# Context columns normed and projected ahead of the latents at three stage entries, with buffers moved to make room

## The chip, the cores and the metric

The kernel runs on one core of one Trainium2 chip. The metric is the device time of one execution in microseconds (us); lower is better. A core has five engines with a queue each: TensorE (PE, matmuls), VectorE (DVE), ScalarE (ACT), GpSimd (POOL) and SyncE (SP, here the stream of weights). Engines meet through semaphores; each works through its own queue in order.

## The reference, cut to what matters

Two models run one after the other. The first block is two layers of five attention branches and ends in a norm; its output `x` (512 tokens, 1024 features) is the "latent" input of the second. The second block also has a "context" of 256 tokens, and every one of its stages begins with the same modulated norm of both:

```python
def _modulate(x, shift, scale):
    return _rms(x) * (1 + scale) + shift

for layer in range(DEPTH):
    h_lat = _modulate(xl, mod_l[0], mod_l[1])
    h_ctx = _modulate(xc, mod_c[0], mod_c[1])
    if layer % 2 == 0:
        y_lat, y_ctx = _conformer_mlstm_mixer(h_lat, h_ctx, ...)   # h @ ab_w_in
    else:
        y_lat, y_ctx = _mla_mixer(h_lat, h_ctx, ...)               # h @ mla_w_in
    xl = xl + mod_l[2] * y_lat
    xl = xl + mod_l[5] * _conv_ffn(_modulate(xl, mod_l[3], mod_l[4]), ffn_w_in[layer], ...)
    if not last:
        xc = xc + mod_c[2] * y_ctx
        xc = xc + mod_c[5] * _conv_ffn(_modulate(xc, mod_c[3], mod_c[4]), ...)
```

The context is known from the start; it changes after the first mixer and after the first FFN, and its projections need its own norm only. So at the entry of the conformer mixer ("AB"), of the first FFN and of the MLA mixer, the context columns do not depend on the last latents.

## The kernel before

Activations lie feature-major: 8 tiles (`k`, KT = 8) of 128 features, each with 768 columns: 256 of context (`BOTH[0]`), then 512 of latents (`BOTH[1]`, `LATENT`). Products in split precision are three matmuls for each pair of tiles (`mm`, L308 to L310): high by high, low by high, high by low. A weight chunk comes by DMA (L416), is cast by ACT to its high half (`Weights.round`, L385) and gets its low half from POOL (`low_parts`, L403, event `weights_low`). PE waits for that event before it uses the chunk. There are NSPLIT = 3 split buffers, so chunk t is cast once chunk t-3 has been used. `round(key, ahead)` casts everything up to `ahead` chunks (AHEAD = 2) beyond the key's, and it stands in ACT's queue where the code calls it: a chunk is never cast before ACT has come to that call.

A stage entry goes like this. DVE adds the residual of the last feature tile (L2058, L2371, L3814), ACT squares it (L492), DVE adds squares (`add_vector`, L500), PE sums over partitions with a matrix of ones in plain fp32 (`sums_tensor`, L307), ACT takes Ln and Exp (L528, L532), DVE does a Newton step (L541 to L550). Then per tile `k`, context first and latents second: DVE scales (`scaled_vector`, L559), ACT makes the high half (`apply_scalar`, L600), DVE the low half (`low_vector`, L571). `apply_scalar` calls `round` for the four chunks ("parts") of the first group after k = 1, 3, 5 and 7. PE follows with `project_group` (or the same loop in `latents_tensor`): three outputs side by side, tile by tile, both column ranges, in four parts of two tiles. At AB the three are gates, g0 and a0, and the next projection is q0; at the FFN they are gate 0, value 0 and gate 1, and the next is value 1; at MLA they are two tiles of the key-value latent and the rope keys (`mla_kr`), and the next is the first query tile (`mla_cq` 0).

What ACT does next in its queue matters too. In `conformer_scalar` it is the sigmoid of g0, an Exp and a Ln of the gates, and then `round` of q0. In `ffn_in_scalar` the first `round` is that of value 1, and it stands at the end of f = 1:

```python
    for f in range(FT):
        ...
        if f > 1:
            g.weights.round(k)
        ... # copy of gate f, wait for the taps of DVE, gelu
        if f > 0:
            g.weights.round(("ffn_value", l, f))
```

In `latents_scalar` it is that of `mla_cq` 0, behind the copies of the first latent and of the rope keys.

PE's accumulators are 8 banks; `claim` waits until the former owner is drained. The final norm of the first block and the latent norm of AB follow each other: the final norm's scaled tiles are squared one by one and summed in 8 fp32 products. The context norm of AB is summed during the last out projection of the first block (`merge_out`), at d = 5. The out products of the FFN (`ffn_out_tensor`) run over the context columns first, then over the latents.

Of the kernel before, what the change touches and what calls it, by code (L numbers as in the profile page):

```python
# [451 lines left out]
class Norm:  # L452
    def __init__(self, key, x, nk, lo, hi, gain, out, sq, dim, shift=None, func=ACT.Identity, rounded=None,
                 added=False, paired=False):
# [67 lines left out]
def root_scalar(g, n):  # L522

    act, S = g.act, g.event
    r = n.sq[:, 1, 0:n.n]
    for m in g.after(act, S("summed").at(n.key)):
        act.wait_ge(*m)
    act.activation(r, g.bank(("sum", n.key), n.nb)[:, 0:n.n], ACT.Ln, bias=g.eps, scale=1.0 / n.dim).then_inc(  # L528
        *S("logarithm").up(act, n.key))
    for m in g.after(act):  # L530
        act.wait_ge(*m)
    act.activation(r, r, ACT.Exp, scale=-0.5).then_inc(*S("root_guessed").up(act, n.key))  # L532


def root_vector(g, n):

    dve, S = g.dve, g.event
    t, r, total = n.sq[:, 0, 0:n.n], n.sq[:, 1, 0:n.n], g.bank(("sum", n.key), n.nb)[:, 0:n.n]
# [14 lines left out]
def scaled_vector(g, n, k):  # L553
# [5 lines left out]
    dve.scalar_tensor_tensor(o, n.x[:, k, n.lo:n.hi], n.gain(k), n.sq[:, 1, 0:n.n], ALU.mult,  # L559
# [27 lines left out]

def apply_scalar(g, *norms, rounds=(), ahead=AHEAD):

    act, S = g.act, g.event  # L590
    for k in range(norms[0].nk):
        for n in norms:
            for m in g.after(act, S("normed").at((n.key, k))):
                act.wait_ge(*m)
            if isinstance(n.out, Split):
                o, high = n.rounded[k % 2][:, 0:n.n], n.out[:, k, n.lo:n.hi].high
                if n.shift is None:
                    act.copy(high, o).then_inc(*S("normed_high").up(act, (n.key, k)))
                else:
                    act.activation(high, o, n.func, bias=n.shift(k)).then_inc(*S("normed_high").up(act, (n.key, k)))  # L600
            else:
                o = n.out[:, k, n.lo:n.hi]
                act.activation(o, o, n.func, bias=n.shift(k)).then_inc(*S("shifted").up(act, (n.key, k)))
        if k % 2 and k // 2 < len(rounds):
            g.weights.round(rounds[k // 2], ahead)

# [1430 lines left out]
def merge_out_scalar(g, l):  # L2037
    act, S, n, last = g.act, g.event, next_norm(g, l), l == DEPTH - 1
    act.preload_act_table_set("natural_log_exp_and_others")
    for d in range(KT):  # L2040
# [6 lines left out]
        if last and d == 5:  # L2047
            root_scalar(g, context_norm(g))
    square_scalar(g, n, KT - 1, [S("drained").at(("merge_out", l, KT - 1))])


def merge_out_vector(g, l):
    dve, S, n = g.dve, g.event, next_norm(g, l)
    for d in range(KT):
# [7 lines left out]
        if l == DEPTH - 1 and d == 5:  # L2062
            root_vector(g, context_norm(g))

# [45 lines left out]
def first_tensor(g):  # L2110
# [26 lines left out]
    sums_tensor(g, final_norm(g), Turn(0, 8))  # L2137
    g.reach(pe, "first_block")


def first_scalar(g):
# [50 lines left out]
    root_scalar(g, n)  # L2192
    for k in range(KT):
# [89 lines left out]
def project_group(g, key, keys, turn, cols, name, lead, x, spans, each, per=2):  # L2283

    pe, n = g.pe, len(keys)
    width = len(cols) // n
    turn.i += turn.i % 2
    for k in keys:
        g.claim(k, turn.next(2), 2)
    for part in range(KT // per):  # L2290
        w, c = g.weights.piece((key, part), name, lead, rows_of(per, part * per * P), cols, split=True)
        for k in range(per):
            kk = part * per + k
            for i, out in enumerate(keys):
                for lo, hi in spans:
                    for m in g.after(pe, each(lo, kk)):
                        pe.wait_ge(*m)
                    done = mm(g, g.wide(out, lo, hi), w[:, k, i * width:(i + 1) * width], x[:, kk, lo:hi], kk == 0,
                              kk == KT - 1)
                if kk == KT - 1:  # L2300
                    done.then_inc(*g.event("projected").up(pe, out))
        if part < KT // per - 1:
            done.then_inc(*g.event("projected").up(pe, (key, part)))
            g.weights.used(c, "projected", (key, part))
        else:
            g.weights.used(c, "projected", keys[-1])
# [10 lines left out]
def modulations(g, l, name, room, shift, scale, with_ctx=True, latent_first=False, added=False):  # L2317
    t, out = g.t, []
    sides = ((1, t.xc, 0, CTX, room.sq_ctx, room.rounded_ctx), (0, t.x, CTX, SEQ, room.sq_lat, room.rounded))
    for side, x, at, n, sq, rounded in sides[0 if with_ctx else 1:]:  # L2320
        out.append(Norm((name, l, side), x, KT, 0, n, lambda k, side=side: mod(g, l, scale, k, side),
                        room.h2[:, :, at:at + n], sq, D_MODEL, rounded=rounded, added=added,
                        shift=lambda k, side=side: mod(g, l, shift, k, side)))
# [37 lines left out]

def residual_vector(g, key, l, which, d, with_ctx=True):
# [21 lines left out]

def conformer_tensor(g, l, norms, turn):
# [8 lines left out]
    project_group(g, "ab_first", [key("gates"), key("g", 0), key("a", 0)], turn,  # L2394
                  np.concatenate([GATES4, ab_cols("g", 0), ab_cols("a", 0)]), "ab_w_in_2", (0,), t.ab.h2, BOTH, each)
# [684 lines left out]

def ab_out_tensor(g, l, turn):
    S = g.event
    for d in range(2, KT):
        project_wide(g, ("ab_out", d), turn, np.arange(d * P, (d + 1) * P), "ab_w_out_2", (0,), g.t.mixed_split, BOTH,
                     lambda lo, k: S("mixed_low").at(k))


def ab_out_scalar(g, l):
# [3 lines left out]
    for d in range(KT):  # L3092
# [3 lines left out]
    residual_squares_scalar(g, norms, KT - 1, [S("drained").at(("ab_out", KT - 1))])  # L3096


def ab_out_vector(g, l):
    dve, S = g.dve, g.event  # L3100
    for d in range(KT):
        residual_vector(g, ("ab_out", d), l, 2, d)
        residual_adds_vector(g, ffn_norms(g, l), d)

# [26 lines left out]
def latents_tensor(g, l, norms, turn):  # L3131
# [7 lines left out]
    turn.i += turn.i % 2  # L3139
    for key, _ in LATENTS:  # L3140
        g.claim(key, turn.next(2), 2)
    for part in range(KT // 2):
        w, c = g.weights.piece(("mla_first", part), "mla_w_in_2", (0,), rows_of(2, part * 2 * P), LATENT_COLS, split=True)
        for k in range(2):
            kk = part * 2 + k
            for key, at in LATENTS:
                for lo, hi in BOTH:
                    for m in g.after(pe, each(lo, kk)):
                        pe.wait_ge(*m)
                    done = mm(g, g.wide(key, lo, hi), w[:, k, at:at + P], t.mla.h2[:, kk, lo:hi], kk == 0, kk == KT - 1)  # L3150
                if kk == KT - 1:
                    done.then_inc(*S("projected").up(pe, key))
# [1186 lines left out]
```

## Time and profile before

| | us |
|---|---|
| median of 3 runs | 3566.45 (3566.43 to 3570.71) |
| the profiled execution | 3567.14 |
| its span in the trace | 3565.8 |
| PE busy | 3361.5 (94%) |
| DVE busy | 1729.6 (49%) |
| ACT busy | 1281.4 (36%) |
| POOL busy | 1021.5 (29%) |

The time of an execution lies 1.3 us above its span. PE's share of busy time is an average over stages; the stage entries are where it is idle. Durations of matmuls in the rows are latencies: they overlap, and the pace is the distance from start to start.

### The profile page before, as it was taken

What the parts mean: (1) busy time and instruction counts of PE and PEld (TensorE: products, weight loads), DVE (VectorE), ACT (ScalarE), POOL (GpSimd) and SP (SyncE); (2) the same over time, 40 slices, a digit from 0 to 9 for tenths busy, and PEclk for the clock granted to TensorE, in tenths of its full rate; (3) what the DMA queues carried; (4) which work ended last, traced back from release to release, by engine and by line L of the source; (5) the groups of instructions that cost most, each with busy time, mean ns of one, the idle gap of its engine ahead of it and who ended that gap; (6) DMA issues with size and microseconds to landing.
All of it is one profiled execution on the core that took longest, in us unless ns stands there. A gap on an engine that the chain in (4) does not pass through costs nothing.

```text
span 3565.8 us, 44523 instructions
## 1 busy us (share of the span) xinstructions
PE 3361.5 (94%) x17208; PEld 2635.6 (74%) x17208; DVE 1729.6 (49%) x3130; ACT 1281.4 (36%) x2198; POOL 1021.5 (29%) x443
## 2 busy tenths in 40 slices
PE   8999999999999999999899889999998988889999
PEld 6677777776867777677687577888987656667877
DVE  5347335434137633534588755222455655543234
ACT  4333323323333332332433443222333445543332
POOL 3123121133302222113235732223453100034443
PEclk9999999999999999999999999999999999999999
DMA  5532121122552122113222001211332110022232
GB/s 180 195 114 83 39 84 60 58 98 104 178 214 73 52 74 76 54 52 133 70 72 77 1 24 54 71 60 62 109 121 74 43 43 1 1 66 95 95 100 77
DMA packets 88340, 288.48 MB, mean 81 GB/s; under 512 B 10048, under 2 KB 20672, under 8 KB 87360
## 3 DMA queue, kind: packets, MB, share of 16 engines
q1 hardware_dynamic: 86832, 274.77, 22.4%
q10 hardware_dynamic: 1296, 10.87, 0.8%
q8 instruction: 136, 2.23, 0.3%
q14 instruction: 76, 0.62, 0.1%
HBM read 281.40 MB, written 4.19 MB: 80 GB/s over the span
## 4 chain that ended last, share of the span: by engine, by line
PE 55%; DVE 6%; ACT 2%; issue 2%; POOL 0%; DVEq 0%; ACTq 0%; POOLq 0%
PE psum L308 14%; PE psum L309 14%; PE psum L310 14%; PE psum L307 11%; PE psum L3448 1%; DVE mla_cols L3537 1%; PE psum L3436 1%; PE psum L1144 1%; DVE h_low L571 1%; DVE padded L2564 0%; DVE ml_weights L2957 0%; PE psum L3414 0%; DVE rounded L559 0%; ACT mla_probs L3493 0%; ACT k_feat L3484 0%
## 5 line engine op out<-in xcount | busy, mean ns | idle before, releaser
L403 POOL TENSOR_TENSOR weights_low<-weights_loaded,weights_high 128x1024 fp32r<-128x1024 f32 (+2 forms) x380 | 910.4, 2396 | 2478.3 <-ACT weights_high L385 2449.1
L308 PE MATMUL psum<-h_high,weights_high 128*128 128x512 f32 (+1 forms) x2400 | 919.9, 383 | 40.7 <-DVE h_low L571 26.5
L309 PE MATMUL psum<-h_low,weights_high 128*128 128x512 f32 (+1 forms) x2400 | 888.5, 370 | 0.0
L310 PE MATMUL psum<-h_high,weights_low 128*128 128x512 f32 (+1 forms) x2400 | 887.7, 370 | 0.0
L308 PEld LDWEIGHTS psum<-h_high,weights_high 128*128 128x128 f32 x2400 | 458.1, 191 | 140.3 <-issue 55.8
L385 ACT CAST weights_high<-weights_loaded 128x1024 fp32r<-128x1024 f32 (+2 forms) x380 | 392.6, 1033 | 462.2 <-PE psum L310 387.5
L309 PEld LDWEIGHTS psum<-h_low,weights_high 128*128 128x128 f32 x2400 | 458.4, 191 | 84.6 <-issue 11.9
L310 PEld LDWEIGHTS psum<-h_high,weights_low 128*128 128x128 f32 x2400 | 457.3, 191 | 78.2
L3804 DVE TENSOR_TENSOR act_low<-ffn_act,act_high 128x512 fp32r<-128x512 f32 (+1 forms) x66 | 142.2, 2154 | 138.5 <-ACT act_high L3774 138.4
L308 PE MATMUL psum<-act_high,weights_high 128*128 128x512 f32 (+1 forms) x528 | 187.8, 356 | 8.4 <-DVE act_low L3804 6.2
L310 PE MATMUL psum<-act_high,weights_low 128*128 128x512 f32 (+1 forms) x528 | 187.5, 355 | 0.0
L309 PE MATMUL psum<-act_low,weights_high 128*128 128x512 f32 (+1 forms) x528 | 187.4, 355 | 0.0
L884 ACT ACTIVATE sig<-psum 128x512 f32<-128x512 f32 x80 | 47.8, 597 | 365.5 <-PE psum L310 341.5
L3686 DVE TENSOR_SCALAR psum<-ffn_row,second 128x770 f32<-128x770 f32 (+1 forms) x44 | 41.7, 949 | 280.5 <-ACT ffn_row L3658 280.4
L307 PE MATMUL psum<-gate,weights_loaded 128*128 128x512 f32 x320 | 155.2, 608 | 3.5 <-ACT gate L656 2.5
L308 PE MATMUL psum<-weights_high,h_high 128*128 128x512 f32 (+3 forms) x432 | 143.7, 333 | 11.2 <-DVE h_low L569 6.1
L309 PE MATMUL psum<-weights_low,h_high 128*128 128x512 f32 (+3 forms) x432 | 141.7, 328 | 0.0
L310 PE MATMUL psum<-weights_high,h_low 128*128 128x512 f32 (+3 forms) x432 | 141.5, 328 | 0.0
L1214 ACT ACTIVATE x<-x,softmax_cols 128x256 f32<-128x256 f32 (+4 forms) x192 | 98.5, 513 | 82.7 <-DVE softmax_cols L1248 77.9
L308 PEld LDWEIGHTS psum<-act_high,weights_high 128*128 128x128 f32 x528 | 100.6, 191 | 23.4 <-issue 5.8
L905 DVE SCALAR_TENSOR_TENSOR sig<-sig,psum 128x512 f32<-128x512 f32 x64 | 44.0, 688 | 149.7 <-PE psum L307 137.3
L2527 DVE SCALAR_TENSOR_TENSOR psum<-padded,second,psum 128x256 f32<-128x256 f32 (+1 forms) x180 | 112.1, 623 | 6.4
(447 smaller groups left out, 5201.2 us busy)
## 6 DMA issues: line engine op xcount, KB each, us to landing
weights_loaded<-stream_dram SPq DMA_DIRECT2D x472, 512.0 KB, 3.3
weights_loaded<-stream_dram SPq DMA_DIRECT2D x80, 128.0 KB, 3.2
weights_loaded<-stream_dram SPq DMA_DIRECT2D x24, 384.0 KB, 3.0
weights_loaded<-stream_dram SPq DMA_DIRECT2D x8, 272.0 KB, 5.5
x<-x_dram SPq DMA_DIRECT2D x4, 512.0 KB, 6.5
arena_mem<-mem_dram ACTq DMA_DIRECT2D x2, 1024.0 KB, 6.7
x<-x_dram ACTq DMA_DIRECT2D x1, 2048.0 KB, 7.7
x_kept_dram<-x ACTq DMA_DIRECT2D x1, 2048.0 KB, 8.7
```

The source lines that it names most:

```text
L307: return pe.matmul(out, a, b, start=start, stop=stop)
L308: pe.matmul(out, a.high, b.high, start=start, stop=False)
L309: pe.matmul(out, a.high, b.low, start=False, stop=False)
L310: return pe.matmul(out, a.low, b.high, start=False, stop=stop)
L385: act.copy(self.high[t % NSPLIT][:, 0:size], self.raw[c % NRAW][:, 0:size]).then_inc(*g.event("weights_high").up(act, c))
L403: pool.tensor_tensor(self.low[s][:, 0:size], raw[:, 0:size], self.high[s][:, 0:size], ALU.subtract).then_inc(*g.event("weights_low").up(po ...
L884: act.activation(g.t.sig[g.sigs.place[key]][:, :], g.bank(key), ACT.Tanh, scale=0.5).then_inc(*S("drained").up(act, key))
L905: dve.scalar_tensor_tensor(dst, s[:, :], 1.0, g.bank(key), ALU.add, ALU.mult).then_inc(*S("drained").up(dve, key))
L1214: act.activation(p[:, h, 0:u.keys], p[:, h, 0:u.keys], ACT.Exp, bias=c[:, 4 + h:5 + h], scale=SCALE, accum_out=None if u.keep is not None ...
L2527: dve.scalar_tensor_tensor(acc, t.up[:, c, at + j:at + j + size], cw[:, j:j + 1], acc, ALU.mult, ALU.add).then_inc(*S("convolved").up(dve, ...
L3686: dve.tensor_scalar(x, r[:, base:base + n], cw[:, 0:1], g.small.ffn_b[l][f], ALU.mult, ALU.add).then_inc(*S("tapped").up(dve))
L3804: dve.tensor_tensor(t.ffn[l].part[i % NPART].low[:, 0:n], t.ffn[l].act[:, f, lo - lo0:lo - lo0 + n], t.ffn[l].part[i % NPART].high[:, 0:n] ...
```

## The change: what it does

At the entries of AB, FFN 0 and MLA the context's norm, its scaling and the first CTX_AHEAD = 3 of 4 parts of the first projection group are moved ahead of the latents' norm. `project_group` becomes a class `Group` with `context(part)`, `latent(part)` and `both(part)`. At AB, DVE scales 6 context tiles in `merge_out` at d = 6, and PE runs `context(0)` before the final norm's sum, `context(1)` and `context(2)` before the latents' sum. At the FFN, the last two out projections of AB are split by side: context columns of both, half of the latents of one, the context's sum, and the rest. At MLA, all 8 context tiles are normed while the FFN's out products of the latents run; bank 7 is held back there for f = 0 and 1 so that the context's sum can use it. In the three places ACT calls `round` after k = 1 and k = 3 of the latents, and once or twice earlier; the calls after k = 5 and 7 are gone. The root of the MLA's context gets a buffer of its own, the fences of PE at `ab_done` and `ffn_done` become marks, and buffers are moved. The second FFN keeps its form.

```diff
+def applied_scalar(g, n, k):       # the body of apply_scalar for one norm and tile
...
+def applied_vector(g, steps):
+    for i, (n, k) in enumerate(steps):
+        scaled_vector(g, n, k)
+        if i:
+            low_vector(g, *steps[i - 1])
+    low_vector(g, *steps[-1])
+CTX_AHEAD = 3
+def early(n):
+    return [(n, k) for k in range(2 * CTX_AHEAD)]
+def late(ctx, lat):
+    return [(lat, k) for k in range(2 * CTX_AHEAD)] + [(n, k) for k in range(2 * CTX_AHEAD, KT) for n in (ctx, lat)]
@@ merge_out_scalar
         if last and d == 5:
             root_scalar(g, context_norm(g))
+        if last and d > 5:
+            for k in range(3 * d - 18, 3 * d - 15):
+                applied_scalar(g, context_norm(g), k)
@@ merge_out_vector
         if l == DEPTH - 1 and d == 5:
             root_vector(g, context_norm(g))
+        if l == DEPTH - 1 and d == 6:
+            applied_vector(g, early(context_norm(g)))
@@ first_tensor
-    sums_tensor(g, final_norm(g), Turn(0, 8))
+    turn = Turn(0, 6)
+    turn.i = 2
+    g.ab_group, sums = ab_group(g, turn), Turn(6, 2)
+    g.ab_group.context(0)
+    sums_tensor(g, final_norm(g), sums)
     g.reach(pe, "first_block")
+    for part in range(1, CTX_AHEAD):
+        g.ab_group.context(part)
+    sums_tensor(g, latent_norm(g), sums)
@@ first_scalar
     root_scalar(g, n)
+    g.weights.round(("ab_first", 0))
@@ class Group
+    def context(self, part):
+        g, pe = self.g, self.g.pe
+        w, _ = self.weights(part)
+        for out, at in zip(self.keys, self.ats):
+            self.claim(out)
+            for k in range(2):
+                kk = 2 * part + k
+                for m in g.after(pe, self.each(0, kk)):
+                    pe.wait_ge(*m)
+                mm(g, g.wide(out, 0, CTX), w[:, k, at:at + P], self.x[:, kk, 0:CTX], kk == 0, kk == KT - 1)
+    def rest(self):
+        for part in range(CTX_AHEAD):
+            self.latent(part)
+        for part in range(CTX_AHEAD, KT // 2):
+            self.both(part)
@@ ab_out_tensor: d = 6 and 7
+def ab_out_apart_tensor(g, turn):
+    ctx, lat = ffn_norms(g, 0)
+    opened, sums = [], Turn(0, 2)
+    for i in range(2):
+        opened.append(ab_out_open(g, AB_APART + i, turn))
+        ab_out_side(g, AB_APART + i, opened[i], BOTH[0], range(KT))
+    ab_out_side(g, AB_APART, opened[0], BOTH[1], range(KT // 2))
+    sums_tensor(g, ctx, sums)
+    ab_out_side(g, AB_APART, opened[0], BOTH[1], range(KT // 2, KT))
+    ab_out_side(g, AB_APART + 1, opened[1], BOTH[1], range(KT))
+    g.reach(g.pe, "ab_done")
...
+    g.ffn_group.context(0)
+    sums_tensor(g, lat, sums)
+    g.reach(g.pe, ("modulated_ffn", 0))
+    for part in range(1, CTX_AHEAD):
+        g.ffn_group.context(part)
+def ab_out_apart_scalar(g):
...
+    root_scalar(g, ctx)
+    square_scalar(g, lat, KT - 2, [S("drained").at(("ab_out", KT - 2))])
+    g.weights.round(first[0], 1)
+    for n, k in early(ctx)[:AB_EARLY]:
+        applied_scalar(g, n, k)
+    square_scalar(g, lat, KT - 1, [S("drained").at(("ab_out", KT - 1))])
+    g.weights.round(first[0])
+    for n, k in early(ctx)[AB_EARLY:]:
+        applied_scalar(g, n, k)
+AB_EARLY = 3
+def ab_out_apart_vector(g):
...
+    applied_vector(g, early(ctx)[:AB_EARLY])
+    residual_side_vector(g, ("ab_out", KT - 1), ("ab_out", KT - 1), 0, 2, KT - 1, 0)
+    applied_vector(g, early(ctx)[AB_EARLY:])
@@ latents_tensor
+    group.context(0)
+    sums_tensor(g, norms[1], Turn(6, 2))
+    g.reach(pe, "modulated_mla")
+    for part in range(1, CTX_AHEAD):
+        group.context(part)
+    group.rest()
     queries(0)
@@ ffn_out_tensor
+            late = with_ctx and side == 0
+            for d in range(KT - 1 if late and f < 2 else KT):
...
+            if late and f == 0:
+                sums_tensor(g, mla_modulations(g)[0], Turn(KT - 1, 1))
@@ ffn_out_scalar
+        if with_ctx and s == FT:
+            root_scalar(g, norms[1])
+        if with_ctx and 0 <= s - FT - MLA_CTX < KT:
+            applied_scalar(g, norms[1], s - FT - MLA_CTX)
     if with_ctx:
-        squares(0)
+        squares(0, [("mla_first", 1), ("mla_first", 2)])
@@ second_scalar
     root_scalar(g, latent_norm(g))
-    apply_scalar(g, context_norm(g), latent_norm(g), rounds=group_parts("ab_first"))
+    for n, k in late(context_norm(g), latent_norm(g)):
+        applied_scalar(g, n, k)
+        if n.key[2] == 0 and k in (1, 3):
+            g.weights.round(("ab_first", k // 2))
     fence_scalar(g, "modulated_ab")
     g.weights.note("conformer")
     conformer_scalar(g, 0)
...
-    modulate_scalar(g, mla_modulations(g), group_parts("mla_first"))
+    ctx, lat = mla_modulations(g)
+    root_scalar(g, lat)
+    for k in range(KT):
+        applied_scalar(g, lat, k)
+        if k in (1, 3):
+            g.weights.round(("mla_first", k // 2))
@@ ffn_scalar
-    modulate_scalar(g, ffn_norms(g, l), group_parts(("ffn_first", l)))
+    first = group_parts(("ffn_first", l))
+    if with_ctx:
+        ctx, lat = ffn_norms(g, l)
+        root_scalar(g, lat)
+        for n, k in late(ctx, lat):
+            applied_scalar(g, n, k)
+            if n is lat and k in (1, 3):
+                g.weights.round(first[k // 2])
+    else:
+        modulate_scalar(g, ffn_norms(g, l), first)
```

## Rows read from the trace of the kernel before

**Rows 1.** Timeline, PE, AB entry: start, us, engine, operation, count [idle before <- releaser].

```profile
1747.02 1.96 PE L307 MATMUL psum<-merged,common 128*128 128x512 f32 x4 [1.67 <-DVE merged L500]
1754.39 9.13 PE L307 MATMUL psum<-squares,common 128*128 128x512 f32 x16 [5.41 <-ACT squares L492]
1769.27 0.55 PE L308 MATMUL psum<-h_high,weights_high 128*128 128x256 f32 x1 [5.76 <-DVE h_low L571]
...
1797.71 0.28 PE L308 MATMUL psum<-h_high,weights_high 128*128 128x256 f32 x1
```

**Rows 2.** Timeline, PE, FFN 0 entry.

```profile
2164.26 3.23 PE L307 MATMUL psum<-squares,common 128*128 128x512 f32 x4
2173.22 0.55 PE L308 MATMUL psum<-h_high,weights_high 128*128 128x256 f32 x1 [5.73 <-DVE h_low L571]
...
2201.39 0.28 PE L308 MATMUL psum<-h_high,weights_high 128*128 128x256 f32 x1
```

**Rows 3.** Timeline, PE, MLA entry.

```profile
2737.25 1.23 PE L307 MATMUL psum<-squares_ctx,common 128*128 128x256 f32 x4 [2.60 <-DVE squares L500]
2738.27 3.49 PE L307 MATMUL psum<-squares,common 128*128 128x512 f32 x4
2747.50 0.55 PE L308 MATMUL psum<-h_high,weights_high 128*128 128x256 f32 x1 [5.73 <-DVE h_low L571]
...
2777.13 0.40 PE L308 MATMUL psum<-h_high,weights_high 128*128 128x512 f32 x1
```

**Rows 4.** Windows of 1 us: stretch, PE, PEld, DVE, ACT, POOL, granted clock, DMA, GB/s.

```profile
1775.00:1776.00 1.00, 1.00 (x6) 0.86 (x5) 0.93 (x3) 0.50 (x1) 0.00 (x0) 0.73 0.31 33
2178.00:2179.00 1.00, 1.00 (x7) 0.91 (x6) 1.00 (x1) 0.00 (x0) 0.81 (x1) 0.85 0.00 0
2751.00:2752.00 1.00, 1.00 (x5) 0.76 (x4) 0.96 (x2) 0.96 (x2) 0.74 (x1) 0.63 0.00 0
```

**Rows 5.** Timeline, PE in the AB group, full clock.

```profile
1775.67 0.28 PE L308 MATMUL psum<-h_high,weights_high 128*128 128x256 f32 x1
...
1776.03 0.40 PE L308 MATMUL psum<-h_high,weights_high 128*128 128x512 f32 x1
...
1776.71 0.28 PE L308 MATMUL psum<-h_high,weights_high 128*128 128x256 f32 x1
```

**Rows 6.** Timeline, DVE, before and in the AB entry.

```profile
1736.49 1.50 DVE L544 TENSOR_TENSOR ml_q<-ml_q 128x256 f32<-128x256 f32 x1
...
1745.46 0.69 DVE L2058 SCALAR_TENSOR_TENSOR x<-psum,x 128x512 f32<-128x512 f32 x1 [4.02 <-PE psum L310]
...
1767.33 0.48 DVE L559 SCALAR_TENSOR_TENSOR rounded_ctx<-context,mods,ml_q 128x256 f32<-128x256 f32 x1
```

**Rows 7.** Timeline, POOL: low halves of a 768- and a 1024-column chunk.

```profile
1735.55 2.15 POOL L403 TENSOR_TENSOR weights_low<-weights_loaded,weights_high 128x768 fp32r<-128x768 f32 x1 [6.25 <-ACT weights_high L385]
...
1804.56 2.40 POOL L403 TENSOR_TENSOR weights_low<-weights_loaded,weights_high 128x1024 fp32r<-128x1024 f32 x1 [1.50 <-issue]
```

**Rows 8.** Timeline, PE, latent half of the FFN's out products, f = 1.

```profile
2620.07 0.50 PE L308 MATMUL psum<-act_high,weights_high 128*128 128x512 f32 x1 [2.22 <-POOL weights_low L403]
```

**Rows 9.** Timeline, ACT, end of the AB entry.

```profile
1792.81 1.05 ACT L385 CAST weights_high<-weights_loaded 128x1024 fp32r<-128x1024 f32 x1
...
1803.38 1.05 ACT L385 CAST weights_high<-weights_loaded 128x1024 fp32r<-128x1024 f32 x1
```

**Rows 10.** Timeline, ACT, after the FFN entry.

```profile
2202.22 0.38 ACT L3655 COPY ffn_row<-psum 128x256 f32<-128x256 f32 x1 [4.24 <-POOL ffn_row L3705]
...
2214.41 2.14 ACT L385 CAST weights_high<-weights_loaded 128x1024 fp32r<-128x1024 f32 x2
```

**Rows 11.** Timeline, ACT, end of the MLA entry.

```profile
2777.38 0.79 ACT L656 COPY k_rope_feat<-psum 32x768 f32<-32x768 f32 x1 [1.27 <-PE psum L310]
2778.20 1.05 ACT L385 CAST weights_high<-weights_loaded 128x1024 fp32r<-128x1024 f32 x1
```

**Rows 12.** Timeline, DVE, conformer: the last of the four products of a and g.

```profile
1898.05 0.42 DVE L2592 TENSOR_TENSOR padded<-psum,sig 128x256 f32<-128x256 f32 x1 [0.60 <-PE psum L310]
```

More of the change, by code:

```diff
@@ L2280, in project_wide, with __init__, weights, products @@
     g.weights.used(c, "projected", key)
[L2283 to L2294, printed above, removed]
+class Group:
+    def __init__(self, g, key, keys, ats, turn, cols, name, lead, x, each):
+        self.g, self.key, self.keys, self.ats, self.turn = g, key, keys, ats, turn
+        self.cols, self.name, self.lead, self.x, self.each = cols, name, lead, x, each
+        self.parts, self.claimed = [], set()
+        turn.i += turn.i % 2
+    def weights(self, part):
+        if part == len(self.parts):
+            self.parts.append(self.g.weights.piece((self.key, part), self.name, self.lead, rows_of(2, 2 * part * P),
+                                                   self.cols, split=True))
+        return self.parts[part]
+    def products(self, part, spans):
+        g, pe = self.g, self.g.pe
+        w, c = self.weights(part)
+        for k in range(2):
+            kk = 2 * part + k
+            for out, at in zip(self.keys, self.ats):
+                self.claim(out)
@@ L2301, in project_group, with claim @@
                     done.then_inc(*g.event("projected").up(pe, out))
-        if part < KT // per - 1:
-            done.then_inc(*g.event("projected").up(pe, (key, part)))
-            g.weights.used(c, "projected", (key, part))
-        else:
-            g.weights.used(c, "projected", keys[-1])
+        return done, c
+    def claim(self, out):
+        if out not in self.claimed:
+            self.claimed.add(out)
+            self.g.claim(out, self.turn.next(2), 2)
+    def context(self, part):
+        g, pe = self.g, self.g.pe
+        w, _ = self.weights(part)
+        for out, at in zip(self.keys, self.ats):
+            self.claim(out)
+            for k in range(2):
+                kk = 2 * part + k
+                for m in g.after(pe, self.each(0, kk)):
+                    pe.wait_ge(*m)
+                mm(g, g.wide(out, 0, CTX), w[:, k, at:at + P], self.x[:, kk, 0:CTX], kk == 0, kk == KT - 1)
@@ L2359, in residual_adds_vector, with residual_side_vector @@
             add_vector(g, n, d - 1)
+def residual_side_vector(g, key, place, l, which, d, side):
+    dve, S = g.dve, g.event
+    x, (lo, hi) = (g.t.xc, BOTH[0]) if side else (g.t.x, BOTH[1])
+    for m in g.after(dve, S("projected").at(key)):
+        dve.wait_ge(*m)
+    dve.scalar_tensor_tensor(x[:, d, :], g.wide(place, lo, hi), mod(g, l, which, d, side), x[:, d, :],
+                             ALU.mult, ALU.add).then_inc(*S("drained").up(dve, key))
 def residual_vector(g, key, l, which, d, with_ctx=True):
@@ new lines, in ab_out_apart_scalar @@
+def ab_out_apart_scalar(g):
+    act, S = g.act, g.event
+    ctx, lat = ffn_norms(g, 0)
+    first = group_parts(("ffn_first", 0))
+    for i in range(2):
+        d = AB_APART + i
+        g.weights.round(("ab_out", d), 1)
+        if not i:
+            residual_squares_scalar(g, (ctx, lat), d - 1, [S("drained").at(("ab_out", d - 1))])
+        square_scalar(g, ctx, d, [S("drained").at(("ab_out_ctx", d))])
+    root_scalar(g, ctx)
[7 more added lines that the diff above has]
+        applied_scalar(g, n, k)
@@ L3137, in queries @@
         project_wide(g, ("mla_cq", j), turn, np.arange(j * P, (j + 1) * P), "mla_w_in_2", (0,), t.mla.h2, LATENT, each)
[L3139 to L3152, printed above, removed]
-        if part < KT // 2 - 1:
-            done.then_inc(*S("projected").up(pe, ("mla_first", part)))
-            g.weights.used(c, "projected", ("mla_first", part))
-        else:
-            g.weights.used(c, "projected", ("mla_kr",))
+    group = Group(g, "mla_first", [key for key, _ in LATENTS], [at for _, at in LATENTS], turn, LATENT_COLS,
+                  "mla_w_in_2", (0,), t.mla.h2, each)
+    group.context(0)
[4 more added lines that the diff above has]
+    group.rest()
     queries(0)
```

211 lines of the change are left out of this document (149 added, 62 removed).

## The prediction

> **What bounds the kernel now.** I read the busy times first: PE is busy for 94% of the span, no other engine for half of it. So a change pays where PE is idle or runs at half its clock, and what sets the time is what PE waits for. The list of PE's waits points to the stage entries; the timeline of each engine across the three entries gives the order, and windows of 1 us the granted clock.
>
> At the AB entry [rows 1] PE waits 1.67 us for the final norm's squares, sums, waits 5.41 us, sums the latents, waits 5.76 us, and only then starts the first group at 1769.27; q0 starts at 1797.71, so the group takes 28.4 us. The FFN entry [rows 2] is alike, 28.2 us, and the MLA entry [rows 3] takes 29.6 us. The clock comes back from 1.2 to 2.4 GHz only about 6.0, 5.0 and 4.2 us into these groups: the stretches that hold the rise are granted 0.73, 0.85 and 0.63 [rows 4]. PE had idled 5.7 us before each group. At half clock those stretches lose 3.0, 2.5 and 2.1 us.
>
> At full clock three matmuls on 256 columns take 0.36 us from start to start and three on 512 take 0.68 [rows 5]. A tile `k` for three outputs is 1.08 us of context and 2.04 of latents.
>
> **What is moved out of the groups.** Three parts are six tiles: 6 x 1.08 = 6.5 us of context work in each entry go to places where PE waits today. What is left is 6 x 2.04 + 2 x 3.12 = 18.5 us at full clock, against 8 x 3.12 = 25.0. DVE takes 0.48 us for a context operation and 0.69 for one on 512 columns [rows 6]; a latent tile needs two, some 1.5 us, under PE's 2.04, so PE sets the pace there.
>
> **AB, up to q0.** DVE now does 12 context operations after the residual of d = 6 and ahead of the residual of d = 7. Merge product 6 ends 24 matmuls, 5.4 us, ahead of 7, near 1740.0; two DVE operations of 0.69 later the twelve begin. They alternate with ACT, which also has a cast and a square in its queue: 12 x 0.52 and 1.0 of waiting, 7.2 us, so they end near 1748.7. The residual of d = 7 stood at 1745.46 [rows 6]; it comes 3.3 us late, and the final sum with it. The cast of part 1, which now sits between ACT's context tiles, releases POOL in the middle of this. While POOL takes its 2.15 us [rows 7], a DVE operation with two SBUF inputs is held: L544 took 1.50 us in place of 0.42 [rows 6]. I add 1.2: final sum +4.5 (bounds 3.3 and 5.5). PE's `context(0)` needs the bank of merge product 7 for its third output and hides in this wait.
>
> The cast of part 2 now stands right after the final norm's Exp, so POOL holds the Newton step, on the path: +1.6 (0 to 2.15). The latents' sum starts 6.1 us late; `context(1)` and `context(2)`, 2.2 us each, run before it, inside a wait of 5.41 us. The 9.13 us of that sum [rows 1] had a slow first half; I take 1.1 off, because PE is busier before it. The first latent low half comes 0.5 us later than the first context one did. Group start: 4.5 + 1.6 - 1.1 + 0.5 = +5.5, at 1774.8. PE idles over 6 us before it, so it starts slow again: 18.5 + 3.0 = 21.5, end 1796.3 against 1797.7: **-1.4** (bounds -3.5 and +1).
>
> **FFN 0, up to value 1.** The context's sum (0.9 us) is added to PE ahead of the last latent product. ACT and DVE hold the last residual up by three context tiles and one POOL operation (1.4 us), then the context tiles 3 to 5 hold up ACT's Ln by 1.1 against 2164.26 + 3.23. With the latent-first order (0.5) the group starts 1.6 us late, 2174.8. `context(0)` fills the wait before the sum, `context(1)` and `(2)` that behind it, which leaves some 3 us idle. I take half of the cold loss, 1.3: 18.5 + 1.3 = 19.8, end 2194.6 against 2201.4: **-6.8** (-8 to -5).
>
> **MLA, up to the first query tile.** All 8 context tiles are normed under the FFN's out products. Their sum falls into a wait that PE has there anyway, 2.22 us before f = 1 [rows 8], and the held-back bank pushes one product of 0.7 us behind that wait: +0.7. At the entry `context(0)` fills the 2.60 us before the sum, the context's sum is gone, and the latents' sum, 3.49 us at half clock [rows 3], runs at full clock, 2.0. Ln comes 2.7 us earlier, the group 2.1 us, at 2745.4; PE idles 2 us before it and should stay fast. 18.5 + 0.5 + 0.7: end 2765.1 against 2777.1: **-12.0** (-13.5 to -9).
>
> So far -1.4 - 6.8 - 12.0 = **-20.2 us**.
>
> **What is late next: the chunk behind the group.** `round` after k = 1 and 3 reaches parts 2 and 3. The calls after k = 5 and 7, which cast the next two chunks before the group ended (the second of them at 1792.81 in AB [rows 9]), are gone, and nothing takes their place until the consumer's own call. PE waits for `weights_low` of that chunk, with everything behind it in its queue.
>
> *AB:* the first call is now where ACT cast at 1803.38 [rows 9], behind the sigmoid, the Exp, the Ln and their table loads, which hang on gates and g0. That is 5.67 us after the group's end. Cast 1.05, hand-over 0.13, POOL 2.40 [rows 7], start 0.1: PE waits 9.3 us. DVE, busy with convolution taps, is no cover: it waits itself for the last a and g [rows 12], and later ones come later by the same.
>
> *FFN:* `round` of value 1 stands behind gelu of f = 1. From the first copy at 2202.22 to the casts at 2214.41 [rows 10] are 12.2 us, and the copy can start 2.0 us before the group's end (today POOL's fill of the rows holds it). 12.2 - 2.0 + 3.65: PE waits 13.9 us. ACT and DVE work meanwhile, but the stage behind is PE's alone, so nothing is given back.
>
> *MLA:* the copy of the rope keys at 2777.38 and then the cast at 2778.20 [rows 11], 1.1 us after the end, + 3.7: 4.8 us.
>
> Together 9.3 + 13.9 + 4.8 = **+28.0 us**. After each wait PE also starts at half clock, as after the idle 5.7 us at the entries: 3.0 + 2.5 + 2.1 = **+7.6** (bounds 0 and 9).
>
> The Trainium skill, "TensorE: Matmul & The Clock Gate", part "What's actually happening", says that the number of cold matmuls varies between runs of one kernel and advises against fitting to a count. No row here tests that. By it the 7.6 would stay out of the sum: +7.8 in place of +15.4.
>
> The holds of DVE by POOL weigh 1.2 + 1.6 at AB. The Trainium skill, "SBUF — State Buffer", section "Who interferes with whom", has a rule against this change: the port pair of the two engines is an exclusive lock for an operation with two SBUF inputs against a GpSimd operation that reads SBUF. The trace agrees (1.50 us for 0.42). Without the lock the sum would be 2.8 lower.
>
> Moved buffers, changed fences: no instruction added. PE's fences there hang on work it waits for anyway; I take 0 (within 1 either way).
>
> **Sum.** -20.2 + 28.0 + 7.6 = +15.4 on the span of 3565.8, which lies 1.3 under its own execution of 3567.14. The median of the runs is 3566.45, so I forecast 3566.45 + 15.4 = about **3582**.
>
> **Rivals.**
> 1. *The chunks are ready in time* (faster). If ACT reached the next cast early enough, say because a call I take as lost still reaches q0, value 1 and `mla_cq` 0, only the -20.2 is left: 3546. It decides the sign once the three waits and their cold starts cost under 20.2 in place of 35.6, 6.7 apiece. For it: PE's work moved is real and the MLA entry alone saves 12. Against it: the order of ACT's queue in the code, and PE's wait for POOL at f = 1 [rows 8], which arises just so. Chance 0.10.
> 2. *The convolution covers AB's wait* (no change). If DVE's convolution taps and not PE set the end of that stage, 9.3 + 3.0 drop out: 3569.5. Against it: DVE waits for PE [rows 12]. Chance 0.10.
> 3. *The clock is not lost at the waits*: PE comes out of them at 2.4 GHz and +7.8 is left, 3574. PE idles longer there than at the entries where it was lost, though the 4.8 us at MLA are a shade shorter. Chance 0.12, half within 0.2%. The clock-gate page's advice, above, would come out here too.
> 4. *The forecast*, all three waits and their slow starts: 0.68, with a range of its own of 3575 to 3591.
>
> **From cases to numbers.** 0.2% is 7.1 us, about what a measurement of this kernel tells from no change: 3559.3 to 3573.6. Faster 0.10; within 0.10 + 0.06 = 0.16, less 0.02 for an AB entry worse than summed: 0.14; slower 0.76. The best bounds of the sum (-25 + 28 + 0) give 3570, the worst (-13 + 28 + 9) 3590. I go from 3567 to 3591.
>
> **What would show it.** Right: PE idle before q0, value 1 and `mla_cq` 0, released by POOL's weights_low, for about 9, 14 and 5 us, each followed by a stretch granted 0.5; groups of 21 to 22, 20 and 19 us; the residual of merge product 7 three or more us behind the product. Wrong: those waits absent or under 3 us; the groups as long as before; DVE rather than PE on the chain through the conformer; the MLA entry not some 12 us shorter.

## The result, and the profile after

The kernel after takes **3593.6 us** (median of 4 runs, 3591.0 to 3596.5), the kernel before 3566.8 beside it: a ratio of 1.007, 95% interval 1.0058 to 1.0083. It is slower, as forecast, but by 26.8 us and not by 15.4, and it lies 2.6 us above the upper end of the range.

The profiled execution took 3596.54 us, its span is 3595.2, 29.4 over that of before. From PE's list of waits for the kernel after, from 1740 to 2860 us (engine, line waited for: us in total, times, longest):

```profile
PE psum L308 <- POOL weights_low L403: 32.2, 5, 13.8
...
PE psum L308 <- DVE h_low L572: 13.2, 5, 6.4
PE psum L308 <- issue: 6.4, 1, 6.4
```

The first line is new in size: in the same stretch of before it was one wait of 2.2 us. Here it holds three long waits (9.08, 13.84 and 4.49 us), one of 2.59 in the AB entry and the old one. The last line is a wait that the prediction doesn't have.

The timeline of PE in the kernel after, all three entries, the rows that answer to [rows 1 to 3]:

```profile
1758.92 2.65 PE L307 MATMUL psum<-merged,common 128*128 128x512 f32 x4
...
1766.31 0.39 PE L308 MATMUL psum<-h_high,weights_high 128*128 128x256 f32 x1 [2.59 <-POOL weights_low L403]
...
1769.56 7.60 PE L307 MATMUL psum<-squares,common 128*128 128x512 f32 x16
1783.55 0.77 PE L308 MATMUL psum<-h_high,weights_high 128*128 128x512 f32 x1 [6.39 <-DVE h_low L572]
...
1813.43 0.58 PE L308 MATMUL psum<-h_high,weights_high 128*128 128x256 f32 x1 [9.08 <-POOL weights_low L403]
...
1915.82 0.82 PE L2504 MATMUL psum<-common,gate_stack 128*128 128x128 f32 x6
1923.00 0.77 PE L308 MATMUL psum<-weights_high,h_high 128*128 128x512 f32 x1 [6.36 <-issue]
...
2201.15 0.80 PE L308 MATMUL psum<-h_high,weights_high 128*128 128x512 f32 x1 [3.70 <-DVE h_low L572]
...
2235.25 0.58 PE L308 MATMUL psum<-h_high,weights_high 128*128 128x256 f32 x1 [13.84 <-POOL weights_low L403]
...
2781.61 0.50 PE L308 MATMUL psum<-h_high,weights_high 128*128 128x512 f32 x1 [2.02 <-DVE h_low L572]
...
2804.95 0.79 PE L308 MATMUL psum<-h_high,weights_high 128*128 128x512 f32 x1 [4.49 <-POOL weights_low L403]
```

PE stands idle for 9.08, 13.84 and 4.49 us before q0, value 1 and `mla_cq` 0. The forecast had 9.3, 13.9 and 4.8. The granted clock behind four of these waits and at the start of two groups (windows: stretch, PE busy, granted clock, DMA, GB/s):

```profile
1813.40:1818.40 5.00, 4.97 (x23) 0.50 0.49 150
1923.00:1928.00 5.00, 5.00 (x12) 0.53 0.00 0
2201.00:2204.00 3.00, 2.85 (x7) 0.50 0.00 0
2235.00:2238.00 3.00, 2.75 (x13) 0.50 0.53 173
2782.00:2785.00 3.00, 3.00 (x15) 1.00 0.01 3
2805.00:2808.00 3.00, 3.00 (x7) 0.50 0.52 175
```

Of the six, only the MLA group starts fast. Beside the first v tile of the conformer, the timeline of before has these rows (PE, then ACT):

```profile
1897.80 0.82 PE L2405 MATMUL psum<-common,gate_stack 128*128 128x128 f32 x6
1899.31 0.47 PE L308 MATMUL psum<-weights_high,h_high 128*128 128x512 f32 x1 [0.69 <-issue]
1903.24 0.80 ACT L2467 COPY mixed_features<-psum 128x768 f32<-128x768 f32 x1 [4.13 <-DVE psum L2527]
1904.08 0.80 ACT L656 COPY ml_cols<-psum 128x768 f32<-128x768 f32 x1
```

and ACT in the kernel after:

```profile
1921.28 0.80 ACT L2566 COPY mixed_features<-psum 128x768 f32<-128x768 f32 x1 [4.13 <-DVE psum L2626]
1922.11 0.80 ACT L684 COPY ml_cols<-psum 128x768 f32<-128x768 f32 x1
```

ACT's two copies stand in the same order, as far behind PE's transposes, in both kernels. But after, PE's first v tile starts at 1923.00, 0.09 us behind the end of the copy of `cols` (1922.11 + 0.80); before, it started 4.8 us ahead of that copy. The releaser is given as "issue", so the cause is read from the code. The change starts the conformer's bank counter at 2. It counts round six banks, so every claim of the conformer moves by two, until the v tiles, which take three. Before, `cols` had banks 0 and 1 and the first v tiles 2, 3 and 4. After, `cols` has 2 and 3; three more don't fit, the counter starts again, and the v tiles claim 0, 1 and 2. Bank 2 is that of `cols`, and only ACT's copy frees it. That copy stands behind the copy of a convolved block, which waits for DVE's taps.

**Where the 29.4 us are.** This compares the two profiled executions. I take the drift (start after less start before) at rows that both traces have; what a slow start costs is how much the drift grows over the matmuls behind it:

- Residual of merge product 6 on DVE, 1747.08 against 1740.02: +7.06, ahead of everything that is moved.
- q0: 1813.43 against 1797.71 [rows 1], +15.72, so 8.66 since then: the wait of 9.08, less 0.42.
- DVE's last product of a and g: 1916.08 against 1898.05 [rows 12], +18.03. The 2.3 more are the slow stretch of 5 us behind the wait.
- First v tile: 1923.00 against 1899.31, +23.69. That is 5.66, and behind it 4.7 us at half clock (granted 0.53 in the 5 us from 1923), which bring the drift to 25.91: 2.2.
- Value 1: 2235.25 against 2201.39 [rows 2], +33.86. Since 25.91 it grew by 7.95: the wait of 13.84, less 5.9. Slow behind it for 3.1 us, which brings 1.45, to 35.31.
- `mla_cq` 0: 2804.95 against 2777.13 [rows 3], +27.82. Since 35.31 that is -7.5: -12.0 and the wait of 4.49. Slow behind it for 3.4 us, 1.7, which makes 29.5; at the end it is 29.4.

### The profile page after: what moved, and what is told of

It reads as the page before. It is cut to its first block, busy times and chain, and to the rows that moved or that the text cites. A ratio compares the mean times of both kernels' runs of the same rounds, so it can differ in the third digit from the quotient of the medians.

```text
span 3595.2 us, 44520 instructions
## 1 busy us (share of the span) xinstructions
PE 3370.3 (94%) x17208; PEld 2647.4 (74%) x17208; DVE 1722.2 (48%) x3130; ACT 1281.9 (36%) x2198; POOL 1021.1 (28%) x443
## 4 chain that ended last, share of the span: by engine, by line
PE 55%; DVE 6%; ACT 3%; issue 2%; POOL 0%; DVEq 0%; ACTq 0%; POOLq 0%
PE psum L308 14%; PE psum L309 14%; PE psum L310 14%; PE psum L307 11%; PE psum L3617 1%; DVE mla_cols L3706 1%; PE psum L3605 1%; PE psum L1172 1%; DVE padded L2663 0%; DVE ml_weights L3056 0%; PE psum L3583 0%; ACT weights_high L385 0%; POOL weights_low L403 0%; ACT mla_probs L3662 0%; ACT k_feat L3653 0%
## 5 line engine op out<-in xcount | busy, mean ns | idle before, releaser
L309 PEld LDWEIGHTS psum<-h_low,weights_high 128*128 128x128 f32 x2400 | 460.2, 192 | 85.3 <-issue 12.4
L4004 DVE TENSOR_TENSOR act_low<-ffn_act,act_high 128x512 fp32r<-128x512 f32 (+1 forms) x66 | 127.8, 1936 | 109.1 <-ACT act_high L3965 108.6
```

Source lines behind the costliest of these rows:

```text
L309: pe.matmul(out, a.high, b.low, start=False, stop=False)
L4004: dve.tensor_tensor(t.ffn[l].part[i % NPART].low[:, 0:n], t.ffn[l].act[:, f, lo - lo0:lo - lo0 + n], t.ffn[l].part[i % NPART].high[:, 0:n] ...
```

## Experiments

Each ratio is to the kernel before, beside it on the same chip.

**1. The calls back.**

```diff
-        if n.key[2] == 0 and k in (1, 3):        # AB; FFN 0 and MLA alike
+        if n.key[2] == 0 and k % 2:
```

> The kernel after, with the two dropped calls of `round` (behind k = 5 and k = 7) back in all three entries. Theory A (the dropped calls cost the three waits for weights_low before q0, value 1 and mla_cq 0, and the slow clock behind each): the waits of 9.1, 13.8 and about 5 us go, with about 7 us of slow clock, so 3593.6 - 35 = about 3559 us. Theory B (only the waits are lost, the clock would have been slow anyway): 3593.6 - 28 = about 3566. Theory C (another unit had set the end behind the waits): less than 15 us gained, over 3578. A wait of about 6.4 us at the first v tile of the conformer should stay in all of them.

Measured: 3565.9 us, ratio 0.9995 (0.9986 to 1.0004); 27.7 less than the kernel after. The three waits are gone and the one before the v tile stays, as the code has it (PE):

```profile
1907.10 0.77 PE L308 MATMUL psum<-weights_high,h_high 128*128 128x512 f32 x1 [6.36 <-issue]
...
2751.63 0.80 PE L308 MATMUL psum<-h_high,weights_high 128*128 128x512 f32 x1 [2.02 <-DVE h_low L572]
```

Theory C falls. By the time, theory B is nearer: 27.7 against the 27.4 of the three waits alone. The profile after has slow starts behind its three waits, and with the waits they are gone; but another has come in their place: the MLA group, which starts fast in the kernel after, starts slow here, behind the same idle time of 2.02 us (windows from 2752):

```profile
2752.00:2755.00 3.00, 3.00 (x8) 0.51 0.01 3
```

The Trainium skill, "TensorE: Matmul & The Clock Gate", part "What's actually happening", says that the number of slow matmuls varies between runs of one kernel. The two windows fit that, though they are of two kernels with the same code ahead of this group, not of two runs of one.

**2. The calls back, and the v tiles on other banks.**

```diff
-        first = turn.next(3)
+        at = ((4, 5, 0), (1, 2, 3))[c]
         for n in range(3):
-            g.claim(key("v", 3 * c + n), first + n)
+            g.claim(key("v", 3 * c + n), at[n])
...
+    turn.i = 0
     projected("o", 2)
```

> As the kernel before it, and the v tiles of the conformer on banks 4, 5, 0 and 1, 2, 3 in place of 0, 1, 2 and 3, 4, 5, so that none of the first three falls on a bank of `cols`, which ACT drains late. Theory A (the claim of the bank of `cols` is what PE waits 6.4 us for, and it restarts slow behind it): 6 to 8 us less than with the calls alone, about 3551. Theory B (the v tiles wait for their weights or for DVE, not for a bank): within 2 us of the calls alone.

Measured: 3554.7 us, ratio 0.9963 (0.9950 to 0.9975), 11.2 less than with the calls alone, somewhat more than the 6 to 8 expected. PE's wait before the first v tile is as in the kernel before:

```profile
1902.86 0.81 PE L2504 MATMUL psum<-common,gate_stack 128*128 128x128 f32 x6
1904.37 0.47 PE L308 MATMUL psum<-weights_high,h_high 128*128 128x512 f32 x1 [0.69 <-issue]
```

Theory A holds. Here the moved work, without the new waits, is faster than before by 12.4 us.

**3. The bank counter alone, in the kernel before.**

```diff
-    conformer_tensor(g, 0, norms, Turn(0, 6))
+    turn = Turn(0, 6)
+    turn.i = 2
+    conformer_tensor(g, 0, norms, turn)
```

> The kernel before, with only the conformer's bank counter started at 2 in place of 0, as the change does. Theory A (banks): +6 to +8 us, 3573 to 3575, and PE idle some 6 us before the first v tile. Theory B (the wait comes from something else in the change): no difference, 3567.

Measured: 3576.1 us, ratio 1.0028 (1.0018 to 1.0039), +9.1 where 6 to 8 were expected. One number is all it takes:

```profile
1913.07 0.77 PE L308 MATMUL psum<-weights_high,h_high 128*128 128x512 f32 x1 [6.36 <-issue]
```

**4. The calls dropped, in the kernel before.**

```diff
-    apply_scalar(..., rounds=group_parts("ab_first"))       # MLA and FFN 0 alike
+    apply_scalar(..., rounds=group_parts("ab_first")[:2])
```

> The kernel before, with only the calls of `round` behind k = 5 and k = 7 dropped at the three entries. Theory A (the calls alone carry the waits and the slow clock behind them): waits of about 9, 14 and 5 us before q0, value 1 and mla_cq 0, and 3566.8 + 28.0 + 7.6 = about 3602 us. Theory B (waits but no loss of clock): 3595. Theory C (the convolution covers the wait in the first entry): 3590.

Measured: 3595.6 us, ratio 1.0079 (1.0066 to 1.0091), +28.6. The waits are those of the kernel after to 0.01 us, though no work is moved (PE):

```profile
1809.66 0.58 PE L308 MATMUL psum<-h_high,weights_high 128*128 128x256 f32 x1 [9.08 <-POOL weights_low L403]
...
2223.89 0.58 PE L308 MATMUL psum<-h_high,weights_high 128*128 128x256 f32 x1 [13.83 <-POOL weights_low L403]
...
2803.31 0.80 PE L308 MATMUL psum<-h_high,weights_high 128*128 128x512 f32 x1 [4.49 <-POOL weights_low L403]
```

Theory A has the waits right and is 6 us too high; C is 6 too low; B (3595) meets the time. But slow starts are there (granted 0.50 in the 3 us behind each wait), and in this execution the mLSTM gives some of it back: the same 200 matmuls (9400 to 9600, counted from the start) last 46.4 us here and 49.8 in the profiled execution of before. Experiment 2, without the new waits, and experiment 6, with the work of before, have 46.4 too, so this is not the wait's doing. It goes with the granted clock (windows, kernel before and then experiment 2; the clock is the number behind POOL's count):

```profile
2027.00:2077.00 50.00, 44.26 (x204) 29.85 (x203) 28.34 (x60) 19.57 (x53) 14.95 (x9) 0.93 0.00 1
```
```profile
2032.00:2079.00 47.00, 41.26 (x206) 28.70 (x205) 29.18 (x60) 19.57 (x53) 13.60 (x8) 1.00 0.00 1
```

**5. The banks left, ACT's copy of `cols` moved.** As experiment 1, and:

```diff
         if c == 2:
+            copy_scalar(g, key("cols"), ...)
             convolved(1)
-    copy_scalar(g, key("cols"), ...)
```

> The kernel after with the calls back, and one thing more: ACT's copy of `cols` stands ahead of its copy of the second convolved block (1) instead of behind it; the banks stay as the change leaves them. Theory A (the v tile waits for a bank that only ACT's late copy of `cols` frees): the wait of 6.4 us before the first v tile goes as it did with other banks, and the time comes down from about 3566 by 8 to 11 us to about 3556. Theory B (PE waits there for DVE's product of the last a and g, or for weights; other banks helped in some other way): no change, 3566.

Measured: 3556.7 us, ratio 0.9970 (0.9959 to 0.9980), 9.2 less than with the calls alone. This undoes the wait from the other side (ACT, then PE):

```profile
1898.31 0.80 ACT L684 COPY ml_cols<-psum 128x768 f32<-128x768 f32 x1
1902.40 0.80 ACT L2566 COPY mixed_features<-psum 128x768 f32<-128x768 f32 x1 [3.29 <-DVE psum L2626]
```
```profile
1899.20 0.47 PE L308 MATMUL psum<-weights_high,h_high 128*128 128x512 f32 x1 [1.44 <-DVE padded L2695]
```

What is left, 1.44 us, is bank 0, which DVE's product of the last a and g frees. With experiments 2 and 3 the cause is shown three ways.

**6. The first block's buffers alone, in the kernel before.**

```diff
-    t.q_even, t.q_odd = sb("queries_even", ..., st), sb("queries_odd", ..., st)
     with ExitStack() as s1:
+        t.merged = sb("merged", ..., s1)
+        t.q_even, t.q_odd = sb("queries_even", ..., s1), sb("queries_odd", ..., s1)
...
-        t.merged = sb("merged", ..., s1)
```

> The kernel before, with only the order of `merged`, `queries_even` and `queries_odd` in the first block's memory changed as the change does. The profiled run after was already 7.1 us behind at the residual of merge product 6, ahead of all moved work. Theory A (the moved buffers make the first block slower): +5 to +8 us, 3572 to 3575. Theory B (the first block varies by as much between executions of one kernel): within 2 us of 3567.

Measured: 3569.1 us, ratio 1.0002 (0.9993 to 1.0011). Theory B: no cost of these buffers is seen, and the interval leaves room for under 4 us. The same follows from the residual of merge product 6 on DVE in the ten profiled executions. With the code of before up to there it starts at 1740.02 (before), 1747.53 (experiment 3), 1743.03 (4) and, with the buffers moved, 1742.41 (6). With that of after: 1747.08 (after), 1741.53 (1), 1744.47 (2), 1740.23 (5), 1749.69 (7) and 1747.84 (8). Both ranges overlap. The 7.06 us are an execution's, not the change's, and before's profiled execution is the fastest of the ten up to there. What differs is the clock (windows, PE alone, before and then after: the same 8118 matmuls keep PE busy for 8.4 us more):

```profile
0.00:1740.02 1740.02, 1655.06 (x8118) 0.98 0.29 101
```
```profile
0.00:1747.08 1747.08, 1663.44 (x8118) 0.97 0.29 101
```

**7. The AB entry mended.** As experiment 2, and (ACT; DVE's tiles are split in the same way):

```diff
-        if last and d > 5:
-            for k in range(3 * d - 18, 3 * d - 15):
+        if last and d == 6:
+            for k in range(3):
                 applied_scalar(g, context_norm(g), k)
     square_scalar(g, n, KT - 1, ...)
+    if last:
+        for k in range(3, 6):
+            applied_scalar(g, context_norm(g), k)
...
+    g.weights.round(("ab_first", 0))
     root_scalar(g, n)
-    g.weights.round(("ab_first", 0))
```

> The kernel with the calls back and the v tiles on other banks (3554.7 us), and in the AB entry two edits: DVE norms only three of the six context tiles ahead of the residual of d = 7 and three behind it, with ACT's square of d = 7 ahead of its last three context tiles; and the cast of part 2 stands ahead of the final norm's Ln, not behind its Exp. Theory A (the residual held by DVE's six tiles, 3.7 us, and the Newton step held by POOL, 1.5 us, are on the path): the final sum starts some 3.5 us earlier, the Newton step takes 0.69 and not 2.17, the group starts 4 to 5 us earlier and the whole is about 3550. Theory B (something else, such as the tiles behind the residual or the squares on ACT, is late next): under 2 us gained, about 3554.

Measured: 3551.3 us, ratio 0.9954 (0.9942 to 0.9967); 3.4 less than experiment 2, which the intervals don't tell from 0. The traces show what moved. In the kernel after, and in experiment 2 alike, the residual of product 7 stood behind the twelve context operations, and two holds are seen on DVE (kernel after):

```profile
1747.08 0.69 DVE L2089 SCALAR_TENSOR_TENSOR x<-psum,x 128x512 f32<-128x512 f32 x1 [1.12 <-PE psum L310]
...
1752.33 2.13 DVE L560 SCALAR_TENSOR_TENSOR ml_cols<-context,mods,ml_q 128x256 f32<-128x256 f32 x1
...
1756.73 0.69 DVE L2089 SCALAR_TENSOR_TENSOR x<-psum,x 128x512 f32<-128x512 f32 x1
...
1764.64 2.17 DVE L551 SCALAR_TENSOR_TENSOR merged<-merged 128x512 f32<-128x512 f32 x1
```

Here (DVE, then PE):

```profile
1749.69 0.69 DVE L2092 SCALAR_TENSOR_TENSOR x<-psum,x 128x512 f32<-128x512 f32 x1 [1.11 <-PE psum L310]
...
1755.14 0.69 DVE L2092 SCALAR_TENSOR_TENSOR x<-psum,x 128x512 f32<-128x512 f32 x1 [0.60 <-PE psum L310]
...
1764.31 0.69 DVE L551 SCALAR_TENSOR_TENSOR merged<-merged 128x512 f32<-128x512 f32 x1
```
```profile
1780.09 0.77 PE L308 MATMUL psum<-h_high,weights_high 128*128 128x512 f32 x1 [6.39 <-DVE h_low L572]
```

From the residual of product 6 to the group it is 30.4 us, against 36.5 in the kernel after, 36.4 in experiment 2 and 29.25 before. So theory A holds at the entry, with 6 us where 4 to 5 were expected, and the first v tile comes 5.6 us earlier than in experiment 2. In the whole time it isn't shown: from the residual to the end the two profiled executions last alike, 1808.4 us here and 1808.8 in experiment 2. Here the 200 matmuls of the mLSTM took 49.8 us and not 46.4, and the MLA group started slow where it was fast there, which together is 5 us.

**8. PE kept busy.** As experiment 7, and matmuls that nobody reads:

```diff
     sums_tensor(g, latent_norm(g), sums)
+    filler(g, final_norm(g), 5)      # 5 matmuls of the ones by x[:, 0, :] into a drained bank
...
         g.ffn_group.context(part)
+    filler(g, ctx, 3)
```

> The kernel with the mended AB entry (3551.3 us), and PE kept busy in the idle time ahead of two groups: 5 matmuls of the ones by x on 512 columns behind the latents' sum in AB, 3 behind context part 2 in FFN 0, into a bank whose sum is drained; their results are read by nobody. Theory A (the idle time of 6.4 and 3.7 us is what lets the clock fall, and the slow start is on the path): the groups start at 2.4 GHz, 2.4 and 1.6 us are won back in stretches of 5 and 3 us, and the whole is about 3547. Theory B (the clock falls there by time or chance, whatever PE does): the same slow start, 3551 or up to 1 more. Theory C (the added matmuls delay the group): its start later by up to 2 us, 3553.

Measured: 3549.2 us, ratio 0.9950 (0.9936 to 0.9963). The 2.1 us less than experiment 7 are under what the runs can tell. In the trace theory A holds for FFN: with 1.13 us idle the group starts at full clock, and in all five other kernels with the work moved (after, experiments 1, 2, 5 and 7), with 3.7 us idle, it starts slow. For AB it holds in small part at most: with 2.10 us idle the group still starts slow, for 3.5 us, where it was 5.1 in experiment 7 and 3.9 to 4.2 in the other four (PE timeline, then windows):

```profile
1771.68 4.46 PE L307 MATMUL psum<-x,common 128*128 128x512 f32 x10
1778.23 0.68 PE L308 MATMUL psum<-h_high,weights_high 128*128 128x512 f32 x1 [2.10 <-DVE h_low L581]
...
2170.33 2.74 PE L307 MATMUL psum<-x,common 128*128 128x512 f32 x6
2174.20 0.50 PE L308 MATMUL psum<-h_high,weights_high 128*128 128x512 f32 x1 [1.13 <-DVE h_low L581]
```
```profile
1778.20:1781.20 3.00, 2.97 (x7) 0.52 0.01 3
2174.00:2177.00 3.00, 2.80 (x12) 1.00 0.00 0
```

Experiment 7's windows at the same places, for comparison:

```profile
1780.00:1785.00 5.00, 4.91 (x12) 0.50 0.01 2
2178.40:2184.40 6.00, 6.00 (x14) 0.50 0.00 0
```

## Why the prediction was wrong, and what in it was right

| step | forecast, us | profile after, us |
|---|---|---|
| AB, up to q0 without its wait | -1.4 | -0.4 |
| FFN 0, up to value 1 without its wait | -6.8 | -5.9, with the mLSTM's part |
| MLA, up to `mla_cq` 0 without its wait | -12.0 | -12.0 |
| the three waits | +28.0 | 9.08 + 13.84 + 4.49 = +27.4 |
| slow clock behind them | +7.6 | 2.3 + 1.45 + 1.7 = +5.5 |
| moved buffers and changed fences | 0 | buffers 0 (experiment 6) |
| conformer's banks | no term | 5.66 + 2.2 = +7.9; measured alone +9.1 |
| first block | no term | +7.1, this execution's |

**The step that failed** is "Moved buffers, changed fences: no instruction added. [...] I take 0 (within 1 either way)". It looked at fences and SBUF, and left out what the new `turn.i = 2` does to every later claim of a PSUM bank. Had the six-bank sequence been written out for the whole conformer, the collision would have shown, and its price too. ACT's copy of `cols` ends at 1904.88 in the trace of before, and PE would have claimed its bank at 1899.31: 5.6 us, and with a slow start behind it, at the 2 us that the least of the entries lost, some 7.6. With that the forecast is 15.4 + 7.6 = +23.0, 3589.5, and the range would have reached above the measured 3593.6. The experiments put the banks at +9.1 and 11.2, with intervals that take in 7.9.

**Two more terms were off, and cancel.** Experiments 1 and 2 split the 26.8 us by medians, which the profiled executions can't do, as their clocks differ:

| term | forecast, us | by medians |
|---|---|---|
| the three entries | -20.2 | -12.4 (experiment 2) |
| the three calls, waits and slow clock | +35.6 | +27.7 (after less experiment 1) |
| conformer's banks | no term | +11.2 (experiment 1 less 2) |

The entries gained 7.8 us less than forecast and the calls cost 7.9 less. These two errors cancel by luck, and so the miss of 11.4 us looks as if it were the banks alone. With only the entries put right the forecast would have been 3590, with only the calls 3574.

**The waits** came to 0.6 us of the forecast and are the whole of the three calls' price in experiments 1 and 4 (27.7 and 28.6 us). **Rival 1** (chunks ready in time) fell: each consumer waited for its chunk. **Rival 2** fell: experiment 4 has the 9.08 and the full price.

**Rival 3**, no clock lost at the waits, is half right. Slow starts behind all three waits are in the trace of after. But the price of the calls in the medians, 27.7 and 28.6, is that of the waits alone. What can be shown is that slow stretches come and go: the MLA group is slow in experiment 1 and fast in the kernel after, and 200 matmuls of the mLSTM took 3.4 us more in before than in experiment 2. Whether the 5.5 us are lost on average stays open; the difference of two medians here is uncertain by some 5 us.

**The entries** were forecast too hopefully. Experiment 2, which has only them, gained 12.4 us and not 20.2, while the trace of after against that of before gives -0.4 - 5.9 - 12.0 = -18.3. Most of that gap is the choice of the execution to compare with. Experiment 6 does the work of before in before's time, and its profiled execution has the 46.4 us in the mLSTM, as experiment 2's has. These two pair better (starts of PE's rows, us):

| | residual of product 6 (DVE) | q0 | value 1 | `mla_cq` 0 | end of the span |
|---|---|---|---|---|---|
| experiment 6 | 1742.41 | 1800.60 | 2199.47 | 2775.07 | 3564.8 |
| experiment 2 | 1744.47 | 1802.78 | 2198.04 | 2763.66 | 3553.3 |

Step by step the moved work changes +0.1, -3.6, -10.0 and -0.1 us: -13.6 together, near the 12.4 of the medians. So AB gained nothing where 1.4 was forecast, FFN 3.6 where 6.8 was, and MLA 10.0 where 12.0 was. It is one pair of executions, and the clock still differs between them in places. In AB the mechanism was as written: DVE's twelve context operations took 8.2 us with POOL's hold (forecast 7.2 + 1.2) and put the residual of product 7 4.2 us back (4.5), the final sum came 4.8 us later (4.5), the Newton step was held for 1.5 (1.6), and the latents' sum was 1.5 shorter (1.1). What was missed is that `context(2)` waits 2.59 us for its low half and then stands in the place of that sum: counted from product 6 the group starts 7.2 us later, where 5.5 was forecast. It then lasts 20.8 us, not 21.5. FFN: the group, forecast at 1.6 us late, starts 2.0 us late, and slow for 3 us. MLA came out as forecast in the profile after, with 2.02 us idle before the group, full clock and -12.0; but in experiments 1, 5 and 7 the same group starts slow, so the full clock is in part luck.

**A faster version.** Moved work, calls back, banks free, AB entry mended: 3551.3 us, 0.9954 of before. With PE kept busy: 3549.2 us, 0.9950 (0.9936 to 0.9963), faster than both kernels, but not told apart from the version without.

## What to carry to other kernels

A counter that hands out buffers in a ring has no local edits: shift its start by two and a claim of three wraps at another place, onto a bank whose reader is late. Write the sequence out to its end. A prefetch call tied to a loop index is a deadline for whoever consumes its data; when a loop is rewritten, count the calls and not only the work. And compare two profiles at common rows from the start on: what differs ahead of the first edit is the executions' own, here 7 us of 29.

## What the runs showed of the hardware

The clock after a short idle time isn't settled by that time alone. Behind 2.02 us of idle PE the MLA group started at full clock in the kernel after and in experiments 2 and 8 (granted 1.00 in the first 3 us) and at half in experiments 1, 5 and 7 (0.50 or 0.51), with the same code ahead of it since the FFN. The first block put merge product 6's residual anywhere from 1740.0 to 1749.7 us in ten executions. Filling 4.46 us of the AB entry's idle time left 2.10 and a slow stretch of 3.5 us, where it was 3.9 to 5.1 unfilled; in FFN, 1.13 us of idle left none.
